# Gate and branch tiles of a two-block transformer kernel: three 256-column products or one of 512 and one of 256

## What is computed

```python
# second block, h = rms_norm(x) of 256 tokens x 1024 features
gate = sigmoid(h @ w_gate + b_gate)            # 2 x 1024 features, one half for each branch
o_sb = stick_breaking_attention(h @ w_in...)   # branch 1, 256 x 1024
o_df = differential_attention(h @ w_in...)     # branch 2, 8 heads, normed per head
y = gate[:, :1024] * (o_sb @ w_br_sb) + gate[:, 1024:] * (o_df @ w_br_df)
x = x + y @ w_out                              # then the gated feed-forward and a final norm
```

## Time and profile before

| what | value |
|---|---|
| median of 3 runs | 844.62 us (843.43 to 844.91) |
| the profiled execution | 844.54 us, of which the span from first to last instruction is 842.7 us |
| PE busy | 801.4 us (95% of the span) |
| DVE busy | 561.2 us (67%) |
| ACT busy | 429.0 us (51%) |
| gate stage, with the attention of 8 heads | about 498 to 573 us of the span |
| first branch | about 573 to 602 us |
| second branch | 602 to 625 us |
| feed-forward | 660 to 830 us |

### The profile page before, as it was taken

One profiled execution on the slowest core, in us unless ns is written; L12 is line 12 of the kernel. 1 busy time (PEld: TensorE's weight loads), 2 busy tenths in 40 slices (PEclk: granted clock), 3 DMA queues, 4 the chain that ended last, 5 costly groups with the idle time before them and its releaser, 6 DMA issues.

```text
span 842.7 us, 13226 instructions
## 1 busy us (share of the span) xinstructions
PE 801.4 (95%) x5114; PEld 698.4 (83%) x5114; DVE 561.2 (67%) x954; ACT 429.0 (51%) x838; POOL 113.6 (13%) x108
## 2 busy tenths in 40 slices
PE   5989999998889899999999999999999999999996
PEld 4768987776789678999988988889997788888885
DVE  5896977846887855346635657775875566566665
ACT  5436647825547544446536535555444445455453
POOL 2243214501532302000000000013001000000000
PEclk9999999999989999999999999999999999999999
DMA  9745411233442235544432534333654637655541
GB/s 313 214 154 170 136 51 35 68 124 111 149 151 101 75 101 174 177 150 149 152 101 85 166 104 146 101 101 100 225 174 129 217 131 234 227 174 190 186 164 51
DMA packets 93502, 121.38 MB, mean 144 GB/s; under 512 B 8760, under 2 KB 69616, under 8 KB 93440
## 3 DMA queue, kind: packets, MB, share of 16 engines
q1 hardware_dynamic: 92432, 117.80, 43.3%
q0 software_dynamic: 432, 1.57, 0.6%
q10 hardware_dynamic: 576, 1.17, 0.4%
HBM read 119.48 MB, written 1.05 MB: 143 GB/s over the span
## 4 chain that ended last, share of the span: by engine, by line
PE 79%; DVE 12%; issue 3%; ACT 1%; POOL 1%; POOLq 0%; DVEq 0%; ACTq 0%
PE banks L415 18%; PE banks L417 17%; PE banks L416 17%; PE banks L459 8%; PE banks L461 3%; DVE w_lo L1495 3%; PE banks L561 1%; DVE small L1589 1%; PE banks L617 1%; PE banks L945 1%; PE banks L422 1%; PE banks L421 1%; PE banks L575 1%; PE banks L520 1%; PE banks L555 1%
## 5 line engine op out<-in xcount | busy, mean ns | idle before, releaser
L1495 DVE TENSOR_TENSOR w_lo<-raw,w_hi 128x1024 fp32r<-128x1024 f32 x216 | 267.6, 1248 | 113.1 <-ACT w_hi L1092 111.1
L1092 ACT CAST w_hi<-raw 128x1024 fp32r<-128x1024 f32 (+1 forms) x217 | 225.2, 1045 | 155.6 <-PE banks L417 111.5
L415 PE MATMUL banks<-h,w_hi 128*128 128x256 f32 (+1 forms) x512 | 150.0, 293 | 2.9 <-DVE w_lo L1495 2.9
L416 PE MATMUL banks<-h,w_hi 128*128 128x256 f32 (+1 forms) x512 | 146.7, 286 | 0.0
L417 PE MATMUL banks<-h,w_lo 128*128 128x256 f32 (+1 forms) x512 | 145.7, 285 | 0.0
L415 PE MATMUL banks<-w_hi,h 128*128 128x512 f32 (+1 forms) x288 | 115.5, 401 | 11.6 <-DVE w_lo L1495 6.7
L417 PE MATMUL banks<-w_hi,h 128*128 128x512 f32 (+1 forms) x288 | 113.1, 393 | 0.0
L416 PE MATMUL banks<-w_lo,h 128*128 128x512 f32 (+1 forms) x288 | 112.8, 392 | 0.0
L415 PEld LDWEIGHTS banks<-h,w_hi 128*128 128x128 f32 x512 | 97.2, 190 | 7.3 <-issue 6.4
L459 PE MATMUL banks<-h,w_hi 128*128 128x512 f32 x288 | 99.1, 392 | 0.0
L417 PEld LDWEIGHTS banks<-h,w_lo 128*128 128x128 f32 x512 | 97.8, 191 | 0.0
(11 more groups left out here) (319 smaller groups left out, 1362.9 us busy)
## 6 DMA issues: line engine op xcount, KB each, us to landing
raw<-in_w_in SPq DMA_DIRECT2D x24, 1024.0 KB, 5.2
raw<-in_a_w_in SPq DMA_DIRECT2D x14, 1024.0 KB, 5.4
raw<-in_w_ffn_gate SPq DMA_DIRECT2D x11, 1024.0 KB, 5.4
raw<-in_w_ffn_up SPq DMA_DIRECT2D x11, 1024.0 KB, 5.4
raw<-in_w_ffn_down SPq DMA_DIRECT2D x11, 1024.0 KB, 5.0
raw<-in_b_w_in SPq DMA_DIRECT2D x9, 1024.0 KB, 5.3
raw<-in_w_gate SPq DMA_DIRECT2D x8, 1024.0 KB, 5.7
raw<-in_a_w_out SPq DMA_DIRECT2D x4, 1024.0 KB, 5.1
```

Source lines behind the costliest of these rows:

```text
L415: mm(o, lh, rh, start=start, stop=False)
L416: mm(o, lh, rl, start=False, stop=False)
L1092: nc.scalar.copy(split(w_hi, s), rawsub(s)[0]).then_inc(S["hi_ready"], 1)
L1495: V.tensor_tensor(split(w_lo, s), rawsub(s)[0], split(w_hi, s).bitcast(F), ALU.subtract).then_inc(S["lo_ready"], 1)
```

## The change

All 32 tiles (16 gate, 8 and 8 branch) now use `wide_tile`. Each has 8 products of 512 columns and 8 of 256 in place of 24 of 256. The second half of each bank is copied by ACT to one of two 256-column buffers in `xn` (`copy_half`), DVE adds the first half (`gate_sum` or `branch_sum`). The tanh of a gate tile is then taken from SBUF, one tile later (`gate_tanh(u - 1)`); the two gated products read SBUF too. `o1_hi` and `o1_lo` become the halves of one tensor.

```diff
             def gate_tile(f):
                 if f < 2:
                     pe.wait_ge(S["fm_dve"], 23 + f)
                 else:
-                    pe.wait_ge(S["gt_t"], f - 1)
-                fm_tile(first["gate"] + f, hq(0), hq(1), ps[f % 2][:, 0:T])
+                    pe.wait_ge(S["g_s"], f - 1)
+                wide_tile(first["gate"] + f, both_parts, hq(0), ps[f % 2][:, :])
...
             def br_sb_tile(f):
                 if f < 2:
-                    pe.wait_ge(S["gt_t"], 15 + f)
+                    pe.wait_ge(S["g_s"], 15 + f)
...
-                fm_tile(first["br_sb"] + f, om(o1_hi), om(o1_lo), ps[f % 4][:, 0:T])
+                wide_tile(first["br_sb"] + f, lambda kt: o1[:, :, kt], om(o1_hi), ps[f % 4][:, :])
...
-                fm_tile(first["br_df"] + f, om(o2_hi), om(o2_lo), ps[f % 4][:, 0:T])
+                wide_tile(first["br_df"] + f, lambda kt: o2[:, :, kt], om(o2_hi), ps[f % 4][:, :])
...
+            def copy_half(n, s, bank):
+
+                act.wait_ge(S["sub_used"], s + 1)
+                if n >= 26:
+                    act.wait_ge(S["y_df"], n - 25)
+                elif n >= 18:
+                    act.wait_ge(S["y_sb"], n - 17)
+                elif n >= 2:
+                    act.wait_ge(S["g_s"], n - 1)
+                nc.scalar.copy(second_half(n), ps[bank][:, T:2 * T]).then_inc(S["g_c"], 1)
+
+            def gate_tanh(u):
+                act.wait_ge(S["g_s"], u + 1)
...
+                A(gth[:, u, :], gth[:, u, :], ACT.Tanh, scale=0.5, bias=hbias[:, u:u + 1]).then_inc(S["gt_t"], 1)
...
                 split_hi_to(first["gate"] + u + RING)
-                act.wait_ge(S["sub_used"], first["gate"] + u + 1)
-                if u == 0:
-                    act.wait_ge(S["pool"], 1)
-                A(gth[:, u, :], ps[u % 2][:, 0:T], ACT.Tanh, scale=0.5, bias=hbias[:, u:u + 1]).then_inc(S["gt_t"], 1)
+                copy_half(u, first["gate"] + u, u % 2)
+                if u:
+                    gate_tanh(u - 1)
...
+            def gate_sum(u):
+                dve.wait_ge(S["g_c"], u + 1)
+                V.tensor_tensor(gth[:, u, :], second_half(u), ps[u % 2][:, 0:T], ALU.add).then_inc(S["g_s"], 1)
+
+            def branch_sum(n, bank):
+                dve.wait_ge(S["g_c"], n + 1)
+                V.tensor_tensor(second_half(n), second_half(n), ps[bank][:, 0:T], ALU.add).then_inc(S["g_s"], 1)
+                dve.wait_ge(S["g_s"], n + 1)
...
                     split_lo_to(first["gate"] + 2 * h + 4)
+                    gate_sum(2 * h)
                     dve.wait_ge(S["d_p"], 2 * h + 2)
...
                     V.tensor_copy(twice[:, :, P + META:P + MP], twice[:, :, P:P + META]).then_inc(S["d_w"], 1)
+                if h < 8:
+                    gate_sum(2 * h + 1)
                 if 1 <= h <= 8:
                     v = h - 1
                     dve.wait_ge(S["d_tr"], v + 1)
...
             def br_sb_gated(f):
-                dve.wait_ge(S["sub_used"], first["br_sb"] + f + 1)
-                V.scalar_tensor_tensor(out=merged[:, f, :], in0=gth[:, f, :], scalar=1.0, in1=ps[f % 4][:, 0:T], op0=ALU.add, op1=ALU.mult)\
+                branch_sum(16 + f, f % 4)
+                V.scalar_tensor_tensor(out=merged[:, f, :], in0=gth[:, f, :], scalar=1.0, in1=second_half(f), op0=ALU.add, op1=ALU.mult)\
                     .then_inc(S["y_sb"], 1)
                 split_lo_to(first["br_sb"] + f + 1 + RING)
```

More of the change, by code:

```diff
@@ L166, in program @@
         h_hi, h_lo = h[:, 0], h[:, 1]
-        o1_hi = sb("o1_hi", [P, KT, T], R)
-        o1_lo = sb("o1_lo", [P, KT, T], R)
+        o1 = sb("o1", [P, 2, KT, T], R)
+        o1_hi, o1_lo = o1[:, 0], o1[:, 1]
         o2 = sb("o2", [P, 2, KT, T], R)
@@ L199, in program @@
             "idsl d_ps d_max d_p d_w d_tr d_wt d_pv d_o lam gt_t odn_sq odn_var odn_rstd odn "
-            "f_c f_s y_sb y_df mg_hi mg_lo f_t f_g f_a f_tr f_hi f_lo fin_ps fin_sq fin_sum fin_rstd fin_x fin_a fin"
+            "f_c f_s g_c g_s y_sb y_df mg_hi mg_lo f_t f_g f_a f_tr f_hi f_lo fin_ps fin_sq fin_sum fin_rstd fin_x fin_a fin"
         ).split():
@@ L314, in both_parts, with second_half @@
             return h[:, :, kt, 0:2 * COL[1]].rearrange("p i (a b) -> p i a b", b=COL[1])[:, :, :, 0:P]
+        def second_half(n):
+            return xn[:, 1536 + T * (n % 2):1536 + T * (n % 2) + T]
         def bc(ap, shape, at):
@@ L1403, in df_squares @@
                     A(xn[:, 1280:1280 + P], odf[:, tt, P * h:P * h + P], ACT.Square, accum_out=osd[:, n:n + 1]).then_inc(S["odn_sq"], 1)
+            def copy_half(n, s, bank):
[9 more added lines that the diff above has]
+                act.wait_ge(S["g_s"], u + 1)
+                if u == 0:
+                    act.wait_ge(S["pool"], 1)
+                A(gth[:, u, :], gth[:, u, :], ACT.Tanh, scale=0.5, bias=hbias[:, u:u + 1]).then_inc(S["gt_t"], 1)
             for u in range(16):
@@ L1414, in _ @@
                 split_hi_to(first["gate"] + u + RING)
-                act.wait_ge(S["sub_used"], first["gate"] + u + 1)
-                if u == 0:
-                    act.wait_ge(S["pool"], 1)
-                A(gth[:, u, :], ps[u % 2][:, 0:T], ACT.Tanh, scale=0.5, bias=hbias[:, u:u + 1]).then_inc(S["gt_t"], 1)
+                copy_half(u, first["gate"] + u, u % 2)
+                if u:
+                    gate_tanh(u - 1)
                 if c == 1 and h >= 3:
                     df_squares(h - 3)
+            gate_tanh(15)
             for h in range(5, 8):
@@ L1423, in _ @@
                 df_squares(h)
-            split_hi_to(first["br_sb"] + 5 + RING)
+                copy_half(11 + h, first["br_sb"] + h - 5, h - 5)
+            for f in range(3, 6):
+                split_hi_to(first["br_sb"] + f + RING)
+                copy_half(16 + f, first["br_sb"] + f, f % 4)
             out_hi(o2_hi)
-            split_hi_to(first["br_sb"] + 7 + RING)
+            for f in range(6, 8):
+                split_hi_to(first["br_sb"] + f + RING)
+                copy_half(16 + f, first["br_sb"] + f, f % 4)
             for f in range(9):
@@ L1429, in _ @@
                     split_hi_to(first["br_df"] + f + RING)
+                    copy_half(24 + f, first["br_df"] + f, f % 4)
                 if f >= 1:
@@ L2100, in _ @@
                     split_lo_to(first["br_df"] + f + RING)
-                    dve.wait_ge(S["sub_used"], first["br_df"] + f + 1)
+                    branch_sum(24 + f, f % 4)
                     t = tmp[:, 1280 + T * (f % 2):1280 + T * (f % 2) + T]
-                    link(V.scalar_tensor_tensor(out=t, in0=gth[:, 8 + f, :], scalar=1.0, in1=ps[f % 4][:, 0:T], op0=ALU.add, op1=ALU.mult))
+                    link(V.scalar_tensor_tensor(out=t, in0=gth[:, 8 + f, :], scalar=1.0, in1=second_half(f), op0=ALU.add, op1=ALU.mult))
                     V.tensor_tensor(merged[:, f, :], merged[:, f, :], t, ALU.add).then_inc(S["y_df"], 1)
```

## The result

The changed kernel takes 848.74 us (median of 7 runs, 847.28 to 849.83) against 844.91 us for the kernel before in the same comparison (7 runs, 843.43 to 846.52). The ratio is 1.0043, with an interval of 1.0030 to 1.0057: slower by 3.8 us. The forecast was 846.9 us, 2.3 us slower, and its range ended at 849.0. Direction and mechanism were right, the size was 1.5 us short.

What follows compares the result with a forecast made beforehand. PE, busy for 95% of the span, bounds the kernel: time falls where its list shortens and rises where it waits. 844.54 + 3.54 - 0.50 - 0.32 + 0.45 - 0.84 gave 846.9 us, range 844.3 to 849.0.

Steps and rivals of the forecast that it cites:

- the race at `d_pv`: Gate stage: PE's tile 2h+1, transposes and scores against ACT and DVE's path; PE waits 0.59 us more a period, +3.54 us.
- The six waits named in advance: Gate stage: PE's weight loads for `d_pv(0)` to `d_pv(5)` wait for DVE's copy, 0.59 us more each.
- Gate tiles: Gate stage: ten tiles outside the stalls gain 0.05 us each, -0.50 us.
- First branch: First branch: tiles 0, 1 and 2 gain 0.105 us each, -0.32 us; DVE's added sums cost +0.45 us.
- DVE's longer list: First branch: six new sums push the low part and the attention output split by 0.51 us; stretch costs +0.45 us.
- Second branch: Second branch: all eight wide tiles take 2.775 us and gain 0.105 us each, -0.84 us.
- Only one half counts: Gate stage rival: ACT's delay is absorbed, DVE's sum is not; 1.8 us in place of 3.54, 845.1 us; chance 0.17.
- Branch tiles not shorter: Branch stages rival: the eleven branch tiles gain nothing from the wide form; 848.0 us; chance 0.06.
- A longer path: Gate stage rival: copy, hop and sum cost 0.9 us a period, 5.4 in place of 3.54; 848.8 us; chance 0.15.
- Faster: Gate and branch rival: `d_pv` is not held up and all 32 tiles gain, 2.5 us; 842.1 us; chance 0.10.

Runs made afterwards that it cites:

- DVE order: Changed kernel with DVE's sum of the odd gate tile moved behind the copies of the transposed weights; 845.97 us, ratio 1.0008 to the kernel before.
- gate tiles only: Changed kernel with both branches' tiles put back to those of the kernel before, only gate tiles wide; 849.32 us, ratio 1.0039 to the kernel before.
- ACT hoist: Changed kernel with ACT's exponentials of u = 2h+1 ahead of the copy and tanh for gate tile 2h; 844.15 us, ratio 0.9988 to the kernel before.
- both edits: Changed kernel with exponentials ahead of ACT's copy and tanh, even sum behind the softmax chain, odd sum behind the weight copies; 843.86 us, ratio 0.9985.
- branch tiles only: Changed kernel with the gate tiles put back to those of the kernel before, only branch tiles wide; 845.44 us, ratio 0.9997 to the kernel before.
- both, with the DVE list: Changed kernel with ACT's exponentials first, both gate sums moved later, and DVE's work around the first branch reordered; 843.12 us, ratio 0.9976.

## Why the prediction was near, and where it failed

**What bounds the kernel, and the race at `d_pv`: right.** The six waits named in advance are the six that grew, and no others of the gate stage. From the start of the ACT instruction that reads tile 2h to the end of the copies the path grew from 4.52 to 5.16 us: 0.31 up to the start of the chain, the rest the sum. With 0.05 us of slack used up (`d_pv` came 0.105 us after the last copy and comes 0.055 after it now), that delays `d_pv` by 0.59 us against tile 2h, as forecast. The step to `d_pv` grew by 0.63 and not by 0.59 because its start moved too: the odd tile in the shadow ends some 0.045 us earlier. A stalled period grew by 0.55 us, against the 0.54 forecast.

**Gate tiles: right.** Ten of them outside the stalls were to gain 0.05 us each. The stage as a whole grew by 3.16 us, the forecast for it was 3.54 - 0.50 = 3.04. The two heads ahead of the first stall show the gain undisturbed: their periods are 9.99 and 7.59 us against 10.04 and 7.68, so 0.05 and 0.09 for two tiles each. Tiles 0 and 1 take 2.80 us and gain only half.

**First branch: right in its net, in part by luck.** Predicted were -0.32 for tiles 0 to 2 and +0.45 for DVE's longer list, +0.13. Measured: +0.16 to the attention transposes; from there tiles 6 and 7 gain 2 x 0.06 and the late split costs 0.14, so +0.18. The list moved as foreseen: the split ended at 602.03 and now ends at 606.79; against the start of `d_pv(7)` (583.86 and 588.22) that is 0.40 us later, where "some 0.5" was said. But tiles 0 to 2 carry the same mis-sized saving as the second branch: at 0.06 us each they bring 0.18 and not 0.32, so DVE's list cost some 0.36 and not 0.45, and the two errors nearly cancel. The order of DVE's list was this cost, since the reordered list gave 0.97 us back in tiles 0 to 5 and 0.18 behind them.

**Second branch: the term that was mis-sized.** "By the same 2.775 us each saves 0.105 us" is the step that failed. A wide tile with `o2` takes 2.82 us, so it saves 0.06, and eight save 0.48 where 0.84 was in the sum. That all eight gain was right: the output projection waits for the last `y_df` only at its third quarter (not the second, as the description of the kernel before has it), and the stretch from its start to the end is unchanged. The text had named both ends (no saving, 0.15) and taken the row it thought nearest; the row was of another stage with another operand. The better reading was in the earlier trace rows itself: the narrow products with `o` already took 0.12 us, those with `h` 0.118. Whatever made them longer was not in the count of products, and there was no ground to let it vanish with the wide form. Carried over as a factor, 2.775 x 0.120 / 0.118 = 2.82 us, it gives the measured value; this was found after the result, and the 2.80 us of other tiles show that the operand is not all of it.

The Trainium skill, page "TensorE: Matmul & The Clock Gate", section on the back-to-back issue gap, has an isolated warm matmul at its columns over 2.4 GHz plus about 2.5 ns; by that a wide tile, 8 x 768 columns and 16 products, is an estimate of 2.60 us. The trace disagrees: 2.775 and 2.82 us. The same section warns that a stream of weight loads and matmuls follows another rule, with about 131 ns for a matmul of 512 columns; the trace disagrees with that as well, at 230 ns and more. By the rows, the same columns take 2.56 us at 2.4 GHz, which leaves 13 to 16 ns a product in wide tiles and 11 to 13 in tiles of 24.

**The sum.** With the measured values the changed stages give +3.16 + 0.18 - 0.46 = +2.88 us against +2.33 predicted: 0.38 of the difference is the second branch, 0.12 the gate stage, 0.05 the first branch. The rest of the +3.8 between the medians isn't in the changed stages.

**The rivals.** "Only one half counts" falls: moving the sum alone gave 2.0 us back and left 0.29 us a period. "Branch tiles not shorter" is half right, as above. "A longer path", at 848.8 us, is the number nearest to the measured 848.74, and for the wrong reason: its 0.9 us a period would have put the gate stage at 80.5 us, and it is 78.72. "Faster" falls with the waits.

## What to carry over

A product form that shortens PE's list and adds a step to two other engines is to be priced by its place in their queues: here a copy (0.27 us of ACT) and a sum (0.34 us of DVE) a period, on engines busy for half and two thirds of the span, made the kernel 3 to 4 us slower, and with the lists put in order it is about 2 us faster. Before such a change is given up, ask what each new step stands in front of. With the exponentials ahead of the copy, the sums behind the copies and the first branch's list put in order, the same change went from 0.4% slower to 0.24% faster than the kernel it started from. A duration taken from another stage is only a bound when the two stages show different times for an operation that both have; here scaling by the two would have come close.

## What the runs showed of the hardware

**The time before the changed code varies with the granted clock.** Ahead of the scores of head 0 the code of both kernels is the same, and the changed kernel's trace is 1.35 us late there. The places can be read. Matched one by one, PE's matmuls are level within 0.1 us up to 120 us, 1.1 us late from 144 to 224 us, and 1.35 to 1.4 us late from 248 us on. Three stretches of 4 us in the kernel before (busy time of PE, PEld, DVE, ACT and POOL, then the granted clock, DMA share, GB/s):

```profile
128.00:132.00 4.00, 3.81 (x35) 2.92 (x35) 3.07 (x9) 3.33 (x14) 2.23 (x4) 1.00 0.01 4
...
230.00:234.00 4.00, 3.47 (x16) 3.50 (x17) 3.97 (x6) 0.00 (x0) 0.00 (x0) 0.50 0.25 64
...
242.00:246.00 4.00, 3.28 (x28) 3.08 (x26) 3.88 (x6) 2.60 (x4) 0.00 (x0) 1.00 0.01 2
```

and in the changed one:

```profile
128.00:132.00 4.00, 4.00 (x33) 3.33 (x32) 2.26 (x7) 2.87 (x13) 1.86 (x3) 0.78 0.00 0
...
230.00:234.00 4.00, 2.40 (x13) 2.43 (x14) 3.97 (x5) 0.30 (x1) 0.00 (x0) 0.77 0.08 9
...
242.00:246.00 4.00, 3.16 (x16) 3.16 (x17) 3.91 (x8) 1.95 (x3) 0.79 (x1) 0.57 0.27 105
```

A mean of 0.57 is a stretch mostly at the lower of the two levels, 1.2 GHz, where it ran at 2.4 before: 16 matmuls in 4 us in place of 28. Around 128 us only the changed kernel's trace has a lower clock, and there it loses 1.1 us. From 228 to 248 us both have it for as long in all, but at other matmuls, and the rest is lost there. PE has idle time ahead of both places (busy for 2.5 of the 4 us from 124 to 128, and 1.7 and 2.7 of the 4 us from 226 to 230). Such pieces fall differently from trace to trace. The six that spend 10.2 us at the lower clock ahead of head 0 start it at 496.9 to 497.7 us, the four that spend 13.7 us there (the changed kernel twice, the DVE order, the gate tiles only) at 498.5 to 499.1. Over the 54 runs of the kernel before, the span goes from 841.6 to 845.4 us; the 8 with a mean clock of 0.989 take 844.5 us on average, the 29 with 0.992 or more 843.1.

**So one trace is a poor ruler for what lies ahead of the change, and the mean over runs a good one.** The mean span of the kernel before is 843.67 us, and its profiled execution, at 842.7, was 0.9 us better than that; that of the changed kernel is 846.79 (14 runs), its profiled one 846.9. This explains about 1.0 of the 1.35 us. The remaining 0.3 us are within the error of the means (spreads of 1.0 and 0.8 us over 54 and 14 runs). The same comparison for every kernel, stages from the scores of head 0 to the end of the span:

| kernel | mean span less that of before, us | change of the stages in the trace, us |
|---|---|---|
| changed kernel (14 runs) | +3.1 | +2.8 |
| DVE order | +0.9 | +0.8 |
| ACT hoist | -1.2 | -0.8 |
| both edits | -1.3 | -0.9 |
| branch tiles only | -0.3 | -0.3 |
| gate tiles only (5 runs) | +3.4 | +3.3 |
| both, with the DVE list | -2.0 | -1.9 |

All seven agree within 0.5 us. The four late traces all have wide gate tiles with ACT's list as in the changed kernel; the fifth such trace, the one whose branch tiles stream `h`, spends 10.2 us at the lower clock and starts head 0 at 497.6. So this form alone doesn't make a trace late. Whether it makes the late pieces more likely is left open; by the means it would be worth about the 0.3 us above, which is within their error.

**The same wide tile takes 2.775 or 2.80 us.** With `h` streamed, products of 512 columns step by 230 ns in the one kind, and by 230 and 236 ns by turns in the other; the 256-column product between two of them takes 114 to 120 ns in both. 512 columns alone are 213 ns at 2.4 GHz. The gate stage of one trace has both kinds, and the same gate tile can be of one kind in one kernel and of the other in the next. With `o2` streamed, the 512-column products of a tile step by 224 to 241 ns, 234 to 236 on the mean, which makes 2.82 us. This is the 0.045 us a tile that the prediction missed; what causes the kinds is open.
